# First attention: the sixteen meta keys of eight heads in one product per tile of tokens, values two turns behind the transposes, retention scores issued by pairs of heads

## The reference, cut to what matters

```python
def attend(args):                       # one block of 128 queries
    s = einsum('bqhd,bkhd->bhqk', qb, k) * scale
    mask = cid[None, :] <= qc[:, None]  # chunk 0 = the 16 meta keys, seen by every query
    p = softmax(where(mask, s, neg), axis=-1)
    return einsum('bhqk,bkhd->bqhd', p, v)
...
s = einsum('bnchd,bnmhd->bnhcm', qc, kc) * intra_decay      # retention
o = intra part of s @ v + cross part from a state per head
o = rms_norm(o, ret_norm) * silu(z)
```

## Time and profile before

| | us |
|---|---|
| median of 3 runs | 1997.31 |
| the profiled execution's own time | 1996.74 |
| its span, first to last instruction | 1995.0 |
| TensorE busy | 1796.6 (90%) |
| VectorE busy | 450.3 (23%) |
| ScalarE busy | 218.1 (11%) |
| mean granted TensorE clock | 0.988 of 2.4 GHz |

### The profile page before, as it was taken

How to read it: one execution, slowest core, us unless ns; L and a number is a source line. 1 busy time by engine, 2 the same in 40 slices (tenths; PEclk the granted TensorE clock), 3 DMA queues, 4 the chain that set the end, 5 groups by cost and what they waited for, 6 DMA issues and landing times.

```text
span 1995.0 us, 20423 instructions
## 1 busy us (share of the span) xinstructions
PE 1796.6 (90%) x8288; PEld 763.0 (38%) x8288; DVE 450.3 (23%) x955; ACT 218.1 (11%) x427; POOL 15.0 (1%) x30
## 2 busy tenths in 40 slices
PE   7999999999999969999888898898988988889887
PEld 4545365453445523333223233232332323323322
DVE  2452254233454232012011010120101201102011
ACT  2131023101255110000000000000000000000000
POOL 0000000000000000000000000000000000000000
PEclk9899999999999989999999999999999999999999
DMA  6101210133122569999999999999999999999998
GB/s 235 60 0 46 79 45 1 55 116 87 53 74 107 219 273 425 425 425 424 426 426 425 425 426 426 424 426 426 426 424 426 426 426 425 426 426 425 426 425 341
DMA packets 82035, 598.53 MB, mean 300 GB/s; under 512 B 8824, under 2 KB 18168, under 8 KB 32712
## 3 DMA queue, kind: packets, MB, share of 16 engines
q1 hardware_dynamic: 81992, 597.93, 72.6%
HBM read 591.38 MB, written 2.10 MB: 297 GB/s over the span
## 4 chain that ended last, share of the span: by engine, by line
DMA 48%; PE 40%; SPq 5%; DVE 3%; ACT 2%; issue 1%; DVEq 0%; ACTq 0%
DMA arena<-in_w 48%; PE PS L1301 15%; PE PS L1809 7%; SPq L417 5%; PE PS L1701 3%; PE PS L1842 2%; PE PS L1468 2%; PE PS L1465 1%; PE PS L1626 1%; PE PS L1454 1%; PE PS L1423 1%; PE PS L1685 1%; PE PS L1776 1%; PE PS L1354 1%; PE PS L1531 1%
## 5 line engine op out<-in xcount | busy, mean ns | idle before, releaser
L1809 PE MATMUL PS<-arena 128*64 128x512 f32 (+1 forms) x3072 | 638.5, 562 | 107.6 <-DMA arena<-in_w 106.8
L1809 PEld LDWEIGHTS PS<-arena 128*64 128x64 f32 x3072 | 208.1, 137 | 538.3 <-issue 355.4
L1842 PE MATMUL PS<-arena 128*64 128x512 f32 x1408 | 323.7, 596 | 24.8 <-ACT arena L750 13.1
L1301 PE MATMUL PS<-arena 128*128 128x512 f32 (+7 forms) x880 | 325.4, 529 | 2.3 <-DVE arena L1042 0.8
L1301 PEld LDWEIGHTS PS<-arena 128*128 128x128 f32 (+1 forms) x880 | 156.3, 193 | 160.7 <-issue 149.6
L1842 PEld LDWEIGHTS PS<-arena 128*64 128x64 f32 x1408 | 114.1, 137 | 224.1 <-issue 166.4
L1266 DVE TENSOR_TENSOR arena<-arena,PS 128x1408 f32<-128x1408 f32 x16 | 25.9, 1621 | 692.9 <-PE PS L1809 692.9
L746 ACT ACTIVATE arena<-PS 128x1408 f32<-128x1408 f32 x16 | 21.5, 1344 | 742.3 <-PE PS L1809 742.3
L1275 DVE COPY arena<-PS 128x512 f32<-128x512 f32 x16 | 11.1, 691 | 328.8 <-PE PS L1842 328.8
L1856 PE MATMUL PS<-arena 64*128 64x512 f32 x256 | 76.7, 626 | 8.9 <-DVE arena L1260 8.1
L1283 DVE TENSOR_TENSOR arena<-arena,PS 128x512 f32<-128x512 f32 x128 | 77.9, 679 | 20.4 <-PE PS L1856 20.4
(11 more groups left out here) (251 smaller groups left out, 1021.0 us busy)
## 6 DMA issues: line engine op xcount, KB each, us to landing
arena<-in_w SPq DMA_DIRECT2D x384, 1408.0 KB, 34.6
arena<-in_w_in SPq DMA_DIRECT2D x5, 2048.0 KB, 7.9
arena<-in_w_in SPq DMA_DIRECT2D x8, 1024.0 KB, 7.0
arena<-in_w_out SPq DMA_DIRECT2D x4, 2048.0 KB, 7.7
arena<-arena SPq DMA_DIRECT2D x64, 67.5 KB, 2.5
arena<-in_tab SPq DMA_DIRECT2D x1, 2304.0 KB
arena<-in_w_in SPq DMA_DIRECT2D x1, 2176.0 KB, 18.6
arena<-in_x SPq DMA_DIRECT2D x4, 512.0 KB, 6.0
```

What stands on the lines that cost most here:

```text
L1301: i = pe.matmul(dst, lhs(k), rhs(k), start=k == 0, stop=k == KD - 1)
L1809: i = pe.matmul(PS[64 * f:64 * f + 64, bank + c // 512, 0:w], XE[:, k, :], slot[:, f * FH + c:f * FH + c + w], start=k == 0, stop=k == KD ...
L1842: ins = pe.matmul(PS[64 * d:64 * d + 64, 6, :], HT[:, j, 64 * f:64 * f + 64], W2R[:, f, j, d * 512:(d + 1) * 512], start=f == 0 and j == 0 ...
```

## The change

The retention scores are issued by pairs: `ret_scores(i)` gives two products, head 2j in rows 0 to 63 and bank 0, head 2j+1 in rows 64 to 127 and bank 1, after every fourth k; it waits for both decays of the pair before. The wait for all twenty decays moves from the end of n = 4 into `ret_mean`, the wait for `e_free` into `ret_out`.

In the attention `norm_p` writes the probabilities of the meta keys of all eight heads of a tile side by side into one 128x128 buffer (`PM`, two of them), by its own small instruction per head. Once per tile, in the turn n % 4 = 3, one transpose turns it; `ptm_out(t)` copies it once per tile. The product of the meta keys is four full 128x128 products per tile against `VM`, a matrix with the meta values of each head in that head's 16 rows and 64 columns and zeros elsewhere. `VM` is made once: a product with a repeated identity (`REP`, made by GpSimd) spreads the meta values over 128 rows, and VectorE multiplies by the mask `own`. `PT` has two buffers, the output of the values alternates between banks 6 and 7 by tile, `values(n-2)` replaces `values(n-1)`, and `tile_out` comes two turns later.

```diff
+            gp.tensor_scalar(REP[0:META, :]..., ident[0:META, 0:META]...to_broadcast([META, MH, META]), 1.0, None, ALU.mult)
...
             def pt_out(n):
-                if n >= 1:
-                    act.wait_ge(s["pv_psum"], n)
-                act.activation(PT[:, :, 0:c], PS[:, 4:6, 0:c], ACT.Copy).then_inc(s["pt_evac"], 1)
+                if n >= 2:
+                    act.wait_ge(s["pv_psum"], n - 1)
+                act.activation(PT[n % 2][:, :, 0:c], PS[:, 4:6, 0:c], ACT.Copy).then_inc(s["pt_evac"], 1)
...
             def ret_decay(i):
-                h, b = i // 5, i % 5
+                h, b = 2 * (i // 10) + i % 2, i // 2 % 5
...
                 for f in range(2):
-                    p = PB[(2 * n + f) % 6][:, 0:c]
-                    i = dve.tensor_scalar(p, p, li[:, f:f + 1], None, ALU.mult)
+                    h = (2 * n + f) % MH
+                    p = PB[(2 * n + f) % 6]
+                    dve.tensor_scalar(PM[n // 4 % 2][:, h * META:(h + 1) * META], p[:, 0:META], li[:, f:f + 1], None, ALU.mult)
+                    i = dve.tensor_scalar(p[:, META:c], p[:, META:c], li[:, f:f + 1], None, ALU.mult)
...
-            def ptm_out(n):
-                dve.wait_ge(s["pt_psum"], n + 1)
-                if n >= 1:
-                    dve.wait_ge(s["pv_psum"], n)
-                dve.tensor_copy(PTM[0:META], PS[0:META, 6, 0:256]...).then_inc(s["ptm_evac"], 1)
+            def vm_out():
+                dve.wait_ge(s["pt_psum"], 1)
+                dve.tensor_tensor(VM..., PS[:, 7, :]..., bc(prm_c("own", 0, MH), VH), ALU.mult).then_inc(s["ptm_evac"], 1)
+            def ptm_out(t):
+                dve.wait_ge(s["pt_psum"], 4 * (t + 1))
+                if t >= 1:
+                    dve.wait_ge(s["pv_psum"], 4 * t)
+                dve.tensor_copy(PTM, PS[:, 6 + (t + 1) % 2, 0:P]).then_inc(s["ptm_evac"], 1)
...
             for n in range(NT * 4):
-                if n >= 1:
-                    ptm_out(n - 1)
+                if n == 2:
+                    vm_out()
+                if n % 4 == 0 and n > 0:
+                    ptm_out(n // 4 - 1)
                 norm_p(n)
                 ...
-                if n % 4 == 0 and n > 0:
+                if n % 4 == 2 and n > 4:
                     tile_out(n // 4 - 1)
                 next(conv, None)
...
-            def ret_score(i):
-                h, b = i // 5, i % 5
-                j, o = h // 2, 64 * (h % 2)
-                if i >= 2:
-                    pe.wait_ge(s["ret_s"], i - 1)
+            def ret_scores(i):
+                j, b = i // 5, i % 5
+                if i >= 1:
+                    pe.wait_ge(s["ret_s"], 2 * i)
...
-                pe.matmul(PS[0:n, i % 2, 0:S - q0], RKT[o:o + 64, j, c:c + n], RQT[o:o + 64, j, q0:S], ...)
+                for f in range(2):
+                    o = 64 * f
+                    pe.matmul(PS[0:n, f, 0:S - q0], RKT[o:o + 64, j, c:c + n], RQT[o:o + 64, j, q0:S], ...)
...
             def ret_mean(j):
                 pe.wait_ge(s["ro_sq"], j + 1)
+                pe.wait_ge(s["ret_s"], 5 * RH)
...
-                    if n < 5 and k % 2 == 1:
-                        ret_score(4 * n + k // 2)
+                    if n < 5 and k % 4 == 3:
+                        ret_scores(2 * n + k // 4)
...
-                if n == 4:
-                    pe.wait_ge(s["ret_s"], 5 * RH)
-                    pe.wait_ge(s["e_free"], 7)
...
             def turn_p(n):
                 if n >= 1:
                     pe.wait_ge(s["pt_evac"], n)
-                    pe.wait_ge(s["ptm_evac"], n)
                 for f in range(2):
                     ...
-                    i = pe.transpose(PS[0:META, 6, f * P:(f + 1) * P], p[:, 0:META], ident)
+                if n % 4 == 3:
+                    pe.wait_ge(s["yo_free"], t) if t >= 1 else pe.wait_ge(s["ptm_evac"], 1)
+                    i = pe.transpose(PS[:, 6 + (t + 1) % 2, 0:P], PM[t % 2], ident)
...
             def values(n):
-                pe.wait_ge(s["ptm_evac"], n + 1)
                 if j == 0 and t >= 1:
-                    pe.wait_ge(s["yo_free"], t)
+                    pe.wait_ge(s["ptm_evac"], t + 1)
+                if j == 0 and t >= 2:
+                    pe.wait_ge(s["yo_free"], t - 1)
                 ...
+                if j == 3:
+                    pe.wait_ge(s["ptm_evac"], t + 2)
+                    for m in range(4):
+                        i = pe.matmul(PS[:, 6 + t % 2, m * P:(m + 1) * P], VM[:, m * P:(m + 1) * P], PTM, start=False, stop=True, ...)
...
+            pe.matmul(PS[:, 7, :], REP[0:META, :], V1[0:META, NT * 512:(NT + 1) * 512], start=True, stop=True)
             for n in range(NT * 4):
                 ...
-                if n >= 1:
-                    values(n - 1)
+                if n >= 2:
+                    values(n - 2)
                 turn_p(n)
+            values(NT * 4 - 2)
             values(NT * 4 - 1)
```

More of the change, by code:

```diff
@@ L84, in _prm_layout @@
                     ("qr", 32), ("qrs", 32), ("kr", 32), ("krs", 32), ("retc", 1),
-                    ("q2", 64), ("q2s", 64), ("k2", 64), ("k2s", 64)):
+                    ("q2", 64), ("q2s", 64), ("k2", 64), ("k2s", 64), ("own", MH)):
         PRM[name] = (at, n)
@@ L230, in build @@
         PB = [BUFA[:, LT * i:LT * (i + 1)] for i in range(4)] + [A[:, QK0 + LT * i:QK0 + LT * (i + 1)] for i in range(2)]
-        PT = A[:, QK0 + 2 * LT:QK0 + 2 * LT + 1024].rearrange("p (f c) -> p f c", f=2)
-        PTM = A[:, QK0 + 2 * LT + 1024:QK0 + 2 * LT + 1280].rearrange("p (f c) -> p f c", f=2)
+        PT = [a.rearrange("p (f c) -> p f c", f=2) for a in (A[:, QK0 + 2 * LT:QK0 + 2 * LT + 1024], SCR)]
+        PM0 = QK0 + 2 * LT + 1024
+        PM = [A[:, PM0 + P * i:PM0 + P * (i + 1)] for i in range(2)]
+        PTM = A[:, PM0 + 256:PM0 + 384]
+        VM = A[:, PM0 + 384:PM0 + 896]
         KRG = c1(160).rearrange("p (t c) -> p t c", t=5)
+        REP = c1(P)
         c2 = Carve(A, KD * LT, YT2_AT)
@@ L1414, in _ @@
                 ret_in(i)
-            def ret_score(i):
-                h, b = i // 5, i % 5
-                j, o = h // 2, 64 * (h % 2)
-                if i >= 2:
-                    pe.wait_ge(s["ret_s"], i - 1)
+            def ret_scores(i):
+                j, b = i // 5, i % 5
+                if i >= 1:
+                    pe.wait_ge(s["ret_s"], 2 * i)
                 c, n = toks(b)
                 q0 = c if b < NT else 0
-                pe.matmul(PS[0:n, i % 2, 0:S - q0], RKT[o:o + 64, j, c:c + n], RQT[o:o + 64, j, q0:S], start=True, stop=True)\
-                    .then_inc(s["rs_psum"], 1)
+                for f in range(2):
+                    o = 64 * f
+                    pe.matmul(PS[0:n, f, 0:S - q0], RKT[o:o + 64, j, c:c + n], RQT[o:o + 64, j, q0:S], start=True, stop=True)\
+                        .then_inc(s["rs_psum"], 1)
             def ret_out(j):
                 pe.wait_ge(s["ret_s"], 10 * j + 10)
+                pe.wait_ge(s["e_free"], 6 + j)
                 for b in range(5):
@@ L1522, in values @@
                 pe.wait_ge(s["pt_evac"], n + 1)
-                pe.wait_ge(s["ptm_evac"], n + 1)
                 if j == 0 and t >= 1:
-                    pe.wait_ge(s["yo_free"], t)
-                for b in range(t + 2):
+                    pe.wait_ge(s["ptm_evac"], t + 1)
+                if j == 0 and t >= 2:
+                    pe.wait_ge(s["yo_free"], t - 1)
+                for b in range(t + 1):
                     for f in range(2):
                         h = 2 * j + f
-                        dst = PS[64 * f:64 * f + 64, 7, j * P:(j + 1) * P]
-                        if b <= t:
-                            i = pe.matmul(dst, V1[:, b * 512 + h * VH:b * 512 + (h + 1) * VH], PT[:, f, b * P:(b + 1) * P],
-                                          start=b == 0, stop=False, skip_group_check=True)
-                        else:
-                            i = pe.matmul(dst, V1[0:META, NT * 512 + h * VH:NT * 512 + (h + 1) * VH], PTM[0:META, f, :],
-                                          start=False, stop=True, skip_group_check=True)
+                        i = pe.matmul(PS[64 * f:64 * f + 64, 6 + t % 2, j * P:(j + 1) * P], V1[:, b * 512 + h * VH:b * 512 + (h + 1) * VH],
+                                      PT[n % 2][:, f, b * P:(b + 1) * P], start=j == 0 and b == 0, stop=False, skip_group_check=True)
+                if j == 3:
+                    pe.wait_ge(s["ptm_evac"], t + 2)
+                    for m in range(4):
+                        i = pe.matmul(PS[:, 6 + t % 2, m * P:(m + 1) * P], VM[:, m * P:(m + 1) * P], PTM, start=False, stop=True, skip_group_check=True)
                 i.then_inc(s["pv_psum"], 1)
@@ L1955 @@
         put(b, rep(swap(w)))
+    put("own", np.arange(P)[:, None] // META == np.arange(MH)[None, :])
     put("retc", np.concatenate([v["ret_norm"][0]] * 2)[:, None])
```

11 lines of the change are left out of this document (7 added, 4 removed).

## The result

| | before | changed |
|---|---|---|
| median of 4 runs each, us | 1997.79 | 1981.88 |
| lowest and highest, us | 1996.18 to 2001.03 | 1981.4 to 1987.43 |
| ratio changed / before | | 0.9926 (95%: 0.9913 to 0.9939) |
| the profiled execution's own time | 1996.74 | 1987.43 |
| its span | 1995.0 | 1985.6 |

The ratio is 14.8 us (12.2 to 17.4) of 1997.8; the medians themselves are 15.9 apart. I had said 13.8 us less and 1983.2 us.

What follows compares the result with a forecast made beforehand. It took a chain of weight transfers (48%) and TensorE (40%) as the bound. Retention 10.5 plus attention 3.3 made 13.8 us less, 1983.2 us; forecast 1981.5 to 1985.5 (chance 0.60), range with rivals 1979 to 1989.5.

Steps and rivals of the forecast that it cites:

- The bound: Whole program: a microsecond taken out before 338 us reaches the end whole, since later work and loads move with it.
- Pairs of scores: Retention: ten pairs overlapping in the two row halves save 7.8 us, ten fewer interruptions 1.9 us.
- Rival C: Retention: the pairs run one after the other, so it gives 4.7 instead of 10.5 us; time 1989, chance 0.07.
- The wait moved: Retention's end: TensorE's 0.77 us stand for the last decay vanishes behind two projections; gain 0.8 us (0.5 to 0.8).
- TensorE's work in the attention: Attention: 9.4 us of meta work removed, 5.5 added, about 4 us less; sixteen new products taken at 4 us.
- Turns 0 to 7: First eight attention turns: VectorE's work plus some 0.2 us waiting per turn, 20.4 against 20.26 us; gain -0.2.
- Turns 8 to 11: Attention: loop of maximum, exponential and division, 3.07 us a turn; 12.65 against 14.29 us, gain 1.6.
- Turns 12 to the end: Attention's tail: loop of 3.6 us for two turns, then TensorE, 0.9 late; 18.8 against 20.68 us, gain 1.9.
- A: Attention gains nothing or loses 1 us, VectorE's loop ruling every turn; time 1986.5 to 1987.5, chance 0.15.
- B: Attention is freed more than thought, gain 6 to 8 us; time 1979 to 1981, chance 0.10.
- D: Attention, turns 0 to 7: TensorE's clock falls to 1.2 GHz, doubling the stage's work, +39 us; about 2025, chance 0.04.

Runs made afterwards that it cites:

- e1: Kernel before with only the retention part (pairs, moved wait), attention as it was; 1986.38 us against 1997.56, ratio 0.9939.
- e2: Changed kernel with score products paired in the old order, eight of ten pairs in the same 64 rows; projections and retention 81.53 us against 74.99.
- e3: Changed kernel with the wait for all twenty decays and e_free put back behind n = 4; projections and retention 76.42 us against 74.99.
- e8: Changed kernel without the four meta-key products per tile (output incomplete); 1.98 us shorter, turns 12 to the end 16.96 us against 18.92.
- e5: Changed kernel with VectorE's small meta-key instruction issued twice per head; 3.36 us longer, turns of tile 2 3.31 us instead of 3.03.
- e6: Changed kernel with the small meta-key instructions behind the row maxima, except in each tile's fourth turn; attention 1.12 us shorter, 50.12 us.
- e4: Changed kernel with values(n-1) in place of values(n-2), the rest kept; attention 53.04 us, 1.80 longer.
- e12: Changed kernel with maxima first, small instructions later, convolution steps in turns 7 to 13 and 15, meta copy behind maxima and division; 1979.69 us, ratio to before 0.9916.
- e10: Changed kernel with the edits of e6 and e7 together; first projection to output projection 126.43 us against the changed kernel's 126.23.
- e7: Changed kernel with the next turn's row maxima ahead of the division, for n below 11; first projection to output projection 126.00 us, 0.23 shorter.
- e9: The changed kernel run again without edits; median 1984.33 us against 2001.15 for the kernel before, ratio 0.9921.

## Why the prediction was right, point by point

- **The bound.** That a microsecond before 338 us reaches the end whole: shown, to within 1.7 us. Over the fourteen profiles of the table, with 17 us between the longest and the shortest whole, the rest is 1656.2 to 1657.9.
- **Pairs of scores**, 7.8 + 1.9: the stage shortened by 10.52 with the wait; a pair of 512 columns takes 1.06, as taken from the earlier trace rows. e1 shows the sum, e2 its division. Rival C is out.
- **The wait moved**, 0.8: right beside the kernel before; e3 shows that with pairs its place is worth 1.43, since it would have grown.
- **TensorE's work in the attention.** A set of four meta products takes 325.84 to 327.00, 1.16 us, where I had 0.9. e8 gives 0.98 each where they count. The Trainium skill's load of 0.107 us ("TensorE: Matmul & The Clock Gate", LDWEIGHTS) wasn't decided by this: eight passes in some 1.0 us are 0.125 each, between it and the recorded 0.193.
- **Turns 0 to 7**, -0.2, measured +0.43: the term that was off. I had added 0.2 us of waiting for the exponential in every turn. VectorE's waits for ScalarE are 4.2 us in seven places in all (the waits shown with the result), and the window shows 19.83 - 19.03 = 0.8 us idle in the eight turns, 0.1 a turn, where I had 1.6. VectorE's own work was 19.0 for 18.9.
- **Turns 8 to 11**, 1.6, measured 1.80, with the loop at 3.04 for 3.07. e5 (+0.28 a turn) and e6 (-0.28 a turn) show that the loop sets the length of these turns.
- **Turns 12 to the end**, 1.9, measured 1.76. e4 gives 1.3 of it to the distance of two turns, e8 shows the meta product in it. The forecast made TensorE 0.9 late; its own terms, 3.8 + 3.9 + 4.8 less 10.75 and 1, give 0.75, so the sum should have been 18.65 and the miss is 0.3.
- **Rivals.** A held that the attention would gain nothing; it gained 4.0, though VectorE rules half of it, as A said. B's 6 to 8 us didn't come with this change; e12 reaches them by other edits, 17.3 us in all less the 10.5. D fell with the clock's 1.00 in this kernel. But its place was well seen: in e10 the clock did fall in turns 0 to 7, for 3.4 us, at a cost of some 0.7 us and not of the 39 that D had for the whole stage. What spoke against D, that gaps of 1.1 us had left the clock at 1.00, doesn't carry over: ahead of the fall in e10 no wait over 0.77 us is marked. That the changed kernel kept its clock was in this sense in part luck.
- **The median** was 1.3 us under the forecast: 0.7 by the attention (3.99 for 3.3), the rest within the spread of the first stretch.

## What to carry to other kernels

Products of 64 rows cost as much alone as in pairs of equal shape in the two halves of the array; issue them in pairs, and look for the wait that grows with them. When an engine's long wait goes, ask which loop is left (here maximum, exponential, division), price it link by link from the rows, and put what isn't part of it behind it. An instruction that waits, here a 0.2 us copy, should stand behind the work that others need; at the head of a turn it held VectorE up to 2.2 us. And read the granted clock of the touched stretch in every profile: e10 joins two edits that each kept it, and lost it.

## What the runs showed of the hardware that was not expected

Two score products of 64 rows, one with 16 and one with 128 columns of weights, took the sum of their single times, in different halves (2.01 us) and in the same half (1.37, both in e2); equal ones took the time of one in different halves (1.06) and saved an entry of 0.2 in the same (1.70). Of these two widths of the weights, then, a pair must have one and the same.

The granted clock fell to 1.2 GHz in the midst of the attention, in e10, with no wait of TensorE over 0.77 us marked ahead of it (the row at 283.13). e7 and the changed kernel, with TensorE busy 1.2 to 1.7 of 2 us in windows of the same turns, kept 1.00.

The first 200 us come in two lengths, some 197 and 201 us, with the same instructions. The timelines start alike and part in the first projections; the kernel before, then e9:

```profile
20.17 36.02 PE L1301 MATMUL PS<-arena 128*128 128x512 f32 x144 [0.45 <-DVE arena L801]
```

```profile
20.17 39.16 PE L1316 MATMUL PS<-arena 128*128 128x512 f32 x144 [0.45 <-DVE arena L807]
```

At their end stand many products of 32 columns, and there the granted clock falls to half in both, 1.2 GHz; in e9 it is at 0.64 from 45 to 50 us where the kernel before has 0.87, and at 0.50 still from 65 to 70 where that has 0.92:

```profile
45.00:50.00 5.00, 5.00 (x42) 5.00 (x41) 0.23 (x1) 0.18 (x1) 0.00 (x0) 0.87 0.77 253
50.00:55.00 5.00, 5.00 (x25) 5.00 (x24) 0.00 (x0) 0.00 (x0) 0.00 (x0) 0.50 0.44 166
...
65.00:70.00 5.00, 5.00 (x12) 2.24 (x11) 0.00 (x0) 0.00 (x0) 0.00 (x0) 0.92 0.00 0
```

```profile
45.00:50.00 5.00, 5.00 (x32) 5.00 (x31) 0.55 (x2) 0.18 (x1) 0.00 (x0) 0.64 0.66 215
50.00:55.00 5.00, 5.00 (x26) 5.00 (x25) 0.00 (x0) 0.00 (x0) 0.00 (x0) 0.50 0.54 204
...
65.00:70.00 5.00, 5.00 (x7) 1.88 (x7) 0.70 (x6) 0.54 (x4) 0.00 (x0) 0.50 0.00 0
```

The fourteen profiles divide by this row: from 65 to 70 us the clock is 0.50 in the five with a first stretch of 200.4 to 201.6 us, and 0.80 to 1.00 in the nine with 196.7 to 198.2; e3, with e9's instructions there, has 0.99. So the spread of 4 us goes with the moment at which the clock falls and comes back. It is more than a quarter of what this change brings, and stages, not totals, tell small changes apart.
